# When the V products of two attention steps are issued together behind the second step's transposes

## The reference

```python
sc = jnp.einsum('bqhd,bqkhd->bhqk', qb, k_sel).astype(jnp.float32) * scale
sc = jnp.where(valid[:, None], sc, NEG)
p = jax.nn.softmax(sc, axis=-1).astype(v.dtype)
return jnp.einsum('bhqk,bqkhd->bqhd', p, v_sel)
```

```python
p_c = masked_softmax(s_c, cmp_end[None, :] <= t[:, None])
o_c = jnp.einsum('bghqn,bngd->bqghd', p_c, v_cmp)
...
p_s = masked_softmax(s_s, ok[:, :, None])
o_s = jnp.einsum('bghqk,bgqkd->bqghd', p_s, v_sel)
...
p_w = masked_softmax(s_w, wmask)
o_w = jnp.einsum('bghqk,bkgd->bqghd', p_w, vwb)
o = gb[..., 0:1] * o_c + gb[..., 1:2] * o_s + gb[..., 2:3] * o_w
```

## Time and profile before

| | |
|---|---|
| median of 3 runs | 1540.86 us (1540.7 to 1541.41) |
| the profiled execution | 1541.43 us, of which the span of the trace is 1539.6 |
| PE busy | 1481.8 us, 96% of the span |
| LDWEIGHTS (PEld) | 1221.7 us, 79% |
| DVE, ACT, POOL busy | 657.7, 620.1, 649.8 us (43%, 40%, 42%) |
| stage "a" | from about 303 to 339 us of the span |
| stage "n" | from about 889 to 1048 us |

### The profile page before, as it was taken

One profiled execution on the slowest core, in us unless ns is written; L12 is line 12 of the kernel. 1 busy time (PEld: TensorE's weight loads), 2 busy tenths in 40 slices (PEclk: granted clock), 3 DMA queues, 4 the chain that ended last, 5 costly groups with the idle time before them and its releaser, 6 DMA issues.

```text
span 1539.6 us, 20811 instructions
## 1 busy us (share of the span) xinstructions
PE 1481.8 (96%) x7827; PEld 1221.7 (79%) x7827; DVE 657.7 (43%) x1381; ACT 620.1 (40%) x1119; POOL 649.8 (42%) x446
## 2 busy tenths in 40 slices
PE   7999999798889999999999889999999999999998
PEld 6888888567657888889897667777888888888886
DVE  4337958357453141421235666662132323332324
ACT  4453654367554222343224456773224222222222
POOL 4333645144332444444332355552444444444442
PEclk9999999999999999999999999999999999999999
DMA  5322432103101333436422100003222222232222
GB/s 184 91 78 91 143 96 81 53 7 91 33 1 42 96 96 96 151 110 201 128 78 81 55 28 1 2 2 123 97 99 91 96 96 96 96 95 95 95 97 94
DMA packets 72521, 130.44 MB, mean 85 GB/s; under 512 B 5799, under 2 KB 29426, under 8 KB 72434
## 3 DMA queue, kind: packets, MB, share of 16 engines
q1 hardware_dynamic: 71730, 127.09, 26.1%
q10 hardware_dynamic: 704, 2.17, 0.4%
HBM read 125.05 MB, written 4.19 MB: 84 GB/s over the span
## 4 chain that ended last, share of the span: by engine, by line
PE 90%; DVE 3%; ACT 3%; issue 2%; POOL 1%; DMA 1%; DVEq 0%; ACTq 0%; POOLq 0%
PE bank L817 71%; PE bank L1027 4%; PE bank L879 4%; PE bank L1019 4%; PE bank L768 3%; PE bank L881 1%; PE bank L1209 1%; PE bank L1064 0%; ACT w_hi L1413 0%; PE bank L1378 0%; DVE q_parts L2189 0%; POOL w_lo L651 0%; DVE proj L2658 0%; POOL sc L684 0%; DMA vec_a<-in_g_mem 0%
## 5 line engine op out<-in xcount | busy, mean ns | idle before, releaser
L651 POOL TENSOR_TENSOR w_lo<-raw,w_hi 128x1024 fp32r<-128x1024 f32 (+4 forms) x222 | 520.2, 2345 | 721.9 <-ACT w_hi L1413 721.6
L1413 ACT ACTIVATE w_hi<-raw 128x1024 fp32r<-128x1024 f32 (+4 forms) x222 | 226.5, 1022 | 612.4 <-DMA raw<-in_w_ff 254.5
L817 PE MATMUL bank<-w_hi,xt_hi 128*128 128x484 f32 (+2 forms) x640 | 240.1, 375 | 2.9 <-POOL w_lo L651 2.9
L817 PE MATMUL bank<-w_lo,xt_hi 128*128 128x484 f32 (+2 forms) x640 | 237.5, 371 | 0.0
L817 PE MATMUL bank<-w_hi,xt_lo 128*128 128x484 f32 (+2 forms) x640 | 237.4, 371 | 0.0
L817 PE MATMUL bank<-xt_hi,w_hi 128*128 128x512 f32 x576 | 228.1, 396 | 1.1 <-issue 1.1
L817 PE MATMUL bank<-xt_hi,w_lo 128*128 128x512 f32 x576 | 225.0, 391 | 0.0
L817 PE MATMUL bank<-xt_lo,w_hi 128*128 128x512 f32 x576 | 224.9, 391 | 0.0
L817 PEld LDWEIGHTS bank<-w_hi,xt_hi 128*128 128x128 f32 x640 | 120.6, 188 | 18.6 <-issue 3.9
L817 PEld LDWEIGHTS bank<-w_hi,xt_lo 128*128 128x128 f32 x640 | 120.6, 188 | 15.0
L817 PEld LDWEIGHTS bank<-w_lo,xt_hi 128*128 128x128 f32 x640 | 120.6, 188 | 14.2
(11 more groups left out here) (349 smaller groups left out, 2338.5 us busy)
## 6 DMA issues: line engine op xcount, KB each, us to landing
raw<-in_w_ff SPq DMA_DIRECT2D x64, 512.0 KB, 3.5
raw<-in_w_in SPq DMA_DIRECT2D x40, 512.0 KB, 3.4
raw<-in_w_in SPq DMA_DIRECT2D x40, 484.0 KB, 3.4
raw<-in_w_in SPq DMA_DIRECT2D x24, 392.0 KB, 3.3
raw<-in_w_out SPq DMA_DIRECT2D x16, 512.0 KB, 3.5
raw<-in_w_branch SPq DMA_DIRECT2D x12, 512.0 KB, 3.6
raw<-in_w_mem_kv SPq DMA_DIRECT2D x8, 512.0 KB, 3.6
raw<-in_w_proj_nsa SPq DMA_DIRECT2D x8, 512.0 KB, 3.4
```

Source lines behind the costliest of these rows:

```text
L651: pool.tensor_tensor(w_lo[:, slot, 0:halves, 0:width], raw[:, slot, 0:halves, 0:width], w_hi[:, slot, 0:halves, 0:width].bitcast(F32), ALU ...
L817: ins = pe.matmul(o, lhs, rhs, start=st and j == 0, stop=en and j == 2)
L1413: act.activation(w_hi[:, slot, 0:halves, 0:width], raw[:, slot, 0:halves, 0:width], ACT.Copy)\
```

## The change

PE no longer issues the V products of "a" and "n" at every position. At even positions it issues none. At odd positions it issues, behind the transposes, those of two steps: of the entry at p - 5 and of the entry at p - 4. The number of products is the same. Stage "n" gets two more homes, six instead of four; stage "a" keeps four. DVE's, ACT's, POOL's and SP's lists keep their order.

```diff
 LAG_T_OF = {"a": 3, "n": 3, "b0": 2, "b1": 2, "m": 2}
+TOGETHER = "an"
...
             elif stage == "n":
-                more = [proj[:, t, W1C + S:W1C + 2 * S] for t in range(2)]
+                more = [proj[:, t, W1C + S:W1C + 2 * S] for t in range(4)]
             return [prob_t[:, k, :] for k in range(2)] + more
...
+        def applied_at(stage, pos):
+
+            if stage not in TOGETHER:
+                both = (pos,)
+            else:
+                both = (pos - 1, pos) if pos % 2 else ()
+            return [p for p in (entry(stage, q) for q in both) if is_step(p)]
...
-                    p = entry(stage, pos - LAG_PV)
-                    if is_step(p):
+                    for p in applied_at(stage, pos - LAG_PV):
                         one, two = 2 * p, 2 * p + 1
                         wait_copied(pe, one)
                         wait_copied(pe, two)
```

## The result

The changed kernel takes 1546.23 us (median of 7 runs, 1546.04 to 1548.32) against 1540.86 (7 runs, 1540.14 to 1541.76): a ratio of 1.0038, 95% interval 1.0027 to 1.005. It is slower by 5.4 us, on the forecast's side and 2 us above its 1544.2, near the upper end of the range of 1541.5 to 1547 that belonged to it. The span of the profiled execution went from 1539.6 to 1545.2 us. Lines moved: V 1027 to 1036, T 1019 to 1028, S 879 to 888, compressed products 1064 to 1073, ACT's copy 1685 to 1693, DVE's copy 2317 to 2325.

What follows compares the result with a forecast made beforehand. PE's order and speed were taken to bound the kernel. New waits for ACT's copies outweigh saved switches: +3.5 us in "n" and -0.2 in "a" give +3.3, 1544.2 on the median's scale; range 1537 to 1549, the forecast's own 1541.5 to 1547.

Steps and rivals of the forecast that it cites:

- row 0 pair: Two positions of "n", the even one in tile row 0: 4.45 us against 4.49 before, with a new wait of 0.32.
- row 1 pair: Two positions of "n", the even one in tile row 1: 5.77 us against 5.34 before, with a new wait of 0.42.
- row 2 pair: Two positions of "n", the even one in tile row 2: 3.34 us against 3.19 before, with a new wait of 0.5.
- row 3 pair: Two positions of "n", the even one in tile row 3: 4.44 us against 4.51 before, with a new wait of 0.3.
- steps 4, 5 and 36, 37: In "n", ACT's copy doesn't move, so the first V group of 12 rows adds 0.65 us, twice: +1.3.
- steps 8 and 9: In "n", a pair behind waits on ACT and DVE, put at no change: 0.
- last three pairs: End of "n", where scores are missing: put at -0.2 us, between -1.1 and +0.9.
- The price of 0.33: Saving in us from joining two steps' V products where both neighbours are of 128*128: 0.18 + 0.15.
- half the waits: Variant of the rival that ACT's copies aren't late: with half the new waits, the time was put at 1536 us.
- The cover: Rival: ACT's copies end no later than PE is ready, so the switches are gained: 1532 us; chance 0.10.
- Gain and waits: Rival: waits 0.1 us shorter at 20 pairs and line 1064 not slowed, total +0.6, 1541.5 us; chance 0.20.
- The clock rival: Rival: PE's new idle time brings half clock in four passes of "n", 1.5 us each: 1550 us; chance 0.10.

Runs made afterwards that it cites:

- e4: Changed kernel with a pass's two compressed products ahead of both joined V groups instead of between them: 1543.78 us, ratio 1.0014.
- e2: V products joined in stage "a" alone, "n" as before but with six homes: 1542.08 us, ratio 1.0005 against the kernel before.
- e13: e4 with ACT's and DVE's copies moved up in "n" from the tenth position, transposes still behind scores: 1540.01 us, ratio 0.9989.
- e10: e7 with ACT's and DVE's copies moved up at the odd positions of "n" too: 1538.96 us, ratio 0.9982.
- e12: Kernel before with ACT's and DVE's copies moved up in "n" from the tenth position, six homes, products and PE order unchanged: 1540.89 us, ratio 0.9996.
- e5: Changed kernel with ACT's copy ahead of the first exponentials at even positions of tile rows 2 and 3 of "n": 1544.12 us, ratio 1.0018.
- e6: Changed kernel with transposes ahead of scores and both copies moved up at even positions of "n" from the tenth: 1546.40 us, ratio 1.0034.
- e7: e6 with the compressed products ahead of both joined V groups as well: 1545.52 us, ratio 1.0023.
- e9: Changed kernel with four homes in "n" instead of six: 1546.93 us, ratio 1.0031.
- e1: V products joined in stage "n" alone, stage "a" as before: 1547.05 us, ratio 1.0036 against the kernel before.

## Why the prediction was right, and where it was off

**The mechanism held.** A position without V leaves only the scores over the copies, and PE waits. From the even position's first scores to the odd one's transposes the forecast had 2.03, 2.35, 2.23 and 2.68 us for tile rows 0 to 3, and the pass above shows just these (1009.44 to 1011.47, 1013.92 to 1016.27, 1019.71 to 1021.94, 1023.08 to 1025.76). By step of the V products, or by tile row of the even position, against the forecast:

| term | forecast, us | measured, us |
|---|---|---|
| row 0 pair: length; four, change | 4.45; -0.16 | 4.48 (1009.44 to 1013.92); -0.03 |
| row 1 pair; six | 5.77; +2.58 | 5.79 (to 1019.71); +2.68 |
| row 2 pair; five | 3.34; +0.75 | 3.37 (to 1023.08); +0.90 |
| row 3 pair; five | 4.44; -0.35 | 4.48 (to 1027.56); -0.42 |
| steps 4, 5 and 36, 37 | +1.3 | +0.74 and +0.65 |
| steps 18 to 21 | -0.66 | -0.69 |
| steps 8 and 9 | 0 | +0.18 |
| steps 22 to 25 | 0 | +0.24 |
| start | +0.2 | +0.08 |
| last three pairs | -0.2 | +0.09 |
| "n" | +3.5 | +4.4 |
| a pass of "a" | -0.14 | -0.30 |

The changes are those of the distance between the first scores of successive even positions, before and after. The row 3 line agrees by luck: four of its five pairs changed by 0.02 or 0.03 where 0.07 each was forecast, and one (from 922.07 before) by 0.31, since it took 4.95 before and not 4.51. Each pair of the full pass is 0.02 to 0.04 longer than forecast, 0.12 a pass: transposes behind a wait cost 0.99 for eight and 0.56 for four, 0.02 and 0.03 more than those that follow scores without a gap. Line 1073's two products behind the switch cost what I took, 1.06 (1017.63 to 1018.69), 0.95 + 0.11, though e4 shows that the 0.11 isn't all the switch's. Of the 0.9 us that "n" took beyond the sum, 0.3 are these small excesses, and 0.4 the steps that I had put at nothing because they lie behind waits on ACT and DVE: the price of a row 2 pair (0.18) was paid at steps 8 and 9 all the same.

**Two slips in the working.** The 0.24 us a place ahead of line 1027's loads isn't the price of a switch: the usual place shows 0.17, and 0.76 stands behind line 1064's long products (1013.82 before). The price of 0.33 didn't use it. And half the waits would give 1538, halfway between 1532 and 1544.2, not 1536.

**The tail of "n" was mis-sized** by 0.3. Where the scores run out, two groups of transposes follow each other with nothing between, and the copies stand bare:

```profile
1045.69 0.87 PE L1028 MATMUL bank<-cst,sc 128*128 128x128 f32 x6
1047.19 1.07 PE L1028 MATMUL bank<-cst,proj 128*128 128x128 f32 x8 [0.63 <-DVE proj L2325]
1048.19 1.53 PE L1036 MATMUL bank<-proj 128*64 128x128 f32 x24
```

Six transposes take 1.50 us to the next start where 0.57 is their work. With V between them before, the six and the eight cost 0.78 and 1.02, 1.80 together, against 2.50 here. The 24 products in one group give back 0.16 of that 0.7. Of the rest 0.45 was given back ahead of it: from the first scores of step 62 to the six transposes it is 4.49 us (1041.20 to 1045.69) against 4.94 before (1035.58 to 1040.52), where these transposes had a wait of 0.35.

**Stage "a" was better than forecast, for a reason worth keeping.** I had held ACT's copy at 1.78 us behind the first score of tile row 0. Rows of the changed kernel, ACT and PE:

```profile
318.08 0.36 ACT L1693 ACTIVATE proj<-bank 128x256 f32<-128x256 f32 x1
```
```profile
316.82 0.49 PE L888 MATMUL bank<-k_t,q_t 64*128 64x128 f32 x4
317.25 0.65 PE L1028 MATMUL bank<-cst,sc 128*128 128x128 f32 x4
317.83 0.70 PE L888 MATMUL bank<-k_t,q_t 64*128 64x256 f32 x4
318.54 0.85 PE L1028 MATMUL bank<-cst,proj 128*128 128x128 f32 x6
...
320.97 1.09 PE L1028 MATMUL bank<-cst,proj 128*128 128x128 f32 x8
321.99 1.13 PE L888 MATMUL bank<-k_t,q_t 64*128 64x512 f32 x4
```

The copy ends at 318.44, 1.62 behind the first score, and PE is ready about then: the scores ahead of the transposes take 0.71 (317.83 to 318.54), 0.64 before, so at most 0.07 is a wait. Before, ACT came to it straight from larger exponentials; the joined group ahead gives ACT the time to be done with them. A queue's backlog doesn't move with the chain; in "n", where ACT was idle ahead of its chain, the same step of reasoning held to 0.01.

At equal clock (e2) the stage is 0.89 us shorter, against -0.2 forecast: four passes give -1.2, so what is left, +0.3, stands against the +0.4 that the forecast had for its end. In the profiled execution of the changed kernel the stage got longer all the same, 37.34 us against 36.80: a stretch of half clock from 308 to 312 us costs 1.43 of it.

The switch price in "a" was as taken. Eight transposes to scores of 64*128 cost 1.02 us (320.97 to 321.99), no less than the 1.02 that they took ahead of V in "a" before (320.49 to 321.51). The Trainium skill says ("TensorEngine Tiling (Array Packing)", Key Properties) that a change of the mode drains the engine. The trace agrees so far as a price at every such change goes; what the engine does in that time it doesn't show.

**The rivals.** The cover did not hold: 11 idle places of PE ahead of transposes between 968 and 1053 us, against one before. Gain and waits did not cancel either, since the waits came at full length. The clock rival, new half clock in the passes of "n", didn't come. "n" has stretches of half clock in both kernels and at about the same places: 0.51 over 897 to 904 and 0.76 over 958 to 965 us before, 0.51 over 898.6 to 905.5 and 0.76 over 959 to 966 after; the passes measured above ran at 1.00. In "a" a new one did come, 0.66 over 307 to 312 us, where before has 1.00. The rule of the Trainium skill ("TensorE: Matmul & The Clock Gate", Part 4: PE-mode transpose) that transposes don't count as PE being busy in the same way made no difference that a run shows: the passes of the changed kernel and of e13 and e10, with transposes and scores alone at even positions, stand at 1.00.

**The rest of the difference.** In the profiled execution "a" ends 0.07 us earlier than before, "n" begins 1.30 later and lasts 4.4 longer, and what follows takes 0.10 less, which makes its 5.6. The 1.37 between the stages arises where the kernel has no edit. There the granted clock is lower after: 0.79 in 864 to 872 us, and 0.76 in 372 to 379, where before has 1.00 in both. I had no term for that. Joining doesn't make the later of the two: e12, whose products are apart, has a clock of 0.91 over 860 to 880 us, as the changed kernel has. So of the 2 us that the forecast lacked only 0.9 is a fault of the sum for "n"; the rest lies outside it, where the single profiles differ in their half clock.

## What to carry to other kernels

Joining visits that cost a fixed switch takes cover from the work in between: list what each engine has queued ahead of the copy or eviction that the next group waits for, and move that copy up first. Look at the second latest releaser as well as the latest: the other engine's copy ended only 0.15 us earlier here, and mending one alone gave less than half of what was expected. A wait priced from the trace of before held in "n", where the releasing engine sat idle ahead of its chain, and not in "a", where it worked off a backlog. Before a difference in span is put down to an edit, compare the stretches of half clock in the two profiles.

## What the runs showed of the hardware

- In "a" eight transposes took 1.02 us ahead of V's 128*64 before the change and 1.02 ahead of scores of 64*128 after it. In "n" they take 0.97 ahead of V and 0.79 ahead of scores, which keep the tile. The rows tell no difference between the two changes.
- PE resumes 0.10 to 0.11 us behind the end of ACT's copy and 0.05 to 0.06 behind DVE's (1020.81 to 1020.86 in e5, 1015.01 to 1015.07 in e10).
- **Half clock moves between executions and kernels, and what moves it is open.** A stretch of half clock in "a" (0.66 over 307 to 312 us) costs 1.43: the stage takes 35.91 or 35.92 us in e2, e6, e7, e9 and e10, and 37.34 to 37.36 in the changed kernel, e4, e5 and e13. It also occurs in e1, whose "a" is that of before (38.3 us against 36.8), so it is not made by the joined order there. The stretch near 373 us was lowered in seven of the ten profiled kernels that join "a" and in none of the four that don't; it costs little (from the end of "a" to the start of "n" e9, with it alone, takes 548.76 us, e2, without, 548.57).
- **The missing gain of "a" may lie in the granted clock.** The 11 executions of e2 have a granted clock of 0.988 to 0.994, 0.991 in the mean; the 26 of the kernel before beside it 0.992 to 0.995, 0.993 in the mean. e2's three fastest, 1538.39 to 1539.02 us, are those at 0.993 and 0.994; its median of 1542.08 is one at 0.988. The order isn't strict, since three at 0.991 take 1542.8 to 1543.5. So joining "a" gains 0.9 us in its stage, and what most executions lose elsewhere goes with a lower clock; that the one causes the other, and why the clock is lower, is not shown.
